# Hybrid attention block: block sums and feature squares move to PSUM and ScalarE, up operands are staged in PSUM, and the first chunk's weights get a buffer of their own

## The reference, cut to what matters

```python
u = rmsnorm(h, attn_norm_g[i])
proj = u @ w_in[i]
...                                   # oA: sliding-window attention, oB: differential attention
h = h + jnp.concatenate([oa, ob], axis=-1) @ w_out[i]
z = rmsnorm(h, mlp_norm_g[i]) @ w_up[i]
h = h + jnp.square(jax.nn.relu(z)) @ w_down[i]
gate = jax.nn.sigmoid(rmsnorm(h, ple_norm_g[i]) @ w_ple_gate[i])
h = h + gate * (p[i] @ w_ple_proj[i])
return rmsnorm(h, final_norm_g)
```

## Time and profile before

| what | value |
|---|---|
| median of 3 runs | 1267.04 us (1265.67 to 1267.32) |
| profiled execution, its own time | 1265.68 us |
| its span | 1263.9 us |
| mean granted PE clock | 0.988 |
| busy: PE, PE weight load, DVE, ACT, POOL | 96%, 76%, 62%, 38%, 48% of the span |
| one chunk, D3 to the next D3 | 81.26 us or 79.65 us |

### The profile page before, as it was taken

The page is one execution under the profiler, slowest core; times in us unless marked ns, Lnnn a source line. Parts: engine busy times, 40 slices in busy tenths (PEclk is TensorE's granted clock), DMA queues, the critical chain, the costliest instruction groups (busy, mean ns, idle before and its releaser), DMA issues.

```text
span 1263.9 us, 14541 instructions
## 1 busy us (share of the span) xinstructions
PE 1211.1 (96%) x5729; PEld 962.7 (76%) x5729; DVE 789.9 (62%) x958; ACT 481.5 (38%) x811; POOL 600.5 (48%) x269
## 2 busy tenths in 40 slices
PE   7999999999999997999999999999999999999997
PEld 5777777777677775778787787877878878888886
DVE  5254556556767597893947939579396693653223
ACT  7344435445555552222322223232232322342223
POOL 3220202222436575645666456654564656375641
PEclk8999999999999998999999999999999999999999
DMA  6811101112612324324234243252422514121203
GB/s 223 277 34 34 34 18 34 35 50 51 198 36 84 117 67 177 139 67 169 97 118 149 67 150 114 84 187 67 150 100 83 199 53 142 41 86 52 63 1 133
DMA packets 104121, 125.72 MB, mean 99 GB/s; under 512 B 21801, under 2 KB 87382, under 8 KB 98678
## 3 DMA queue, kind: packets, MB, share of 16 engines
q1 hardware_dynamic: 103814, 124.18, 30.1%
q10 hardware_dynamic: 240, 0.62, 0.1%
HBM read 111.14 MB, written 16.01 MB: 101 GB/s over the span
## 4 chain that ended last, share of the span: by engine, by line
PE 45%; DVE 10%; issue 5%; DMA 1%; POOL 0%; ACT 0%; SPq 0%; DVEq 0%; ACTq 0%
PE ps L1713 36%; PE ps L1374 8%; DVE block_raw L2337 4%; DVE h L2366 2%; DVE block_raw L2320 1%; DVE block_raw L2317 1%; PE ps L1398 1%; DVE w_raw L2262 1%; DMA raw_x<-in_w_up 1%; PE ps L1870 0%; PE ps L1412 0%; DVE diag L1957 0%; PE ps L1701 0%; POOL w_lo L832 0%; ACT w_hi L958 0%
## 5 line engine op out<-in xcount | busy, mean ns | idle before, releaser
L736 POOL TENSOR_TENSOR w_lo<-w_raw,w_hi 128x1024 fp32r<-128x1024 f32 x38 | 96.6, 2543 | 271.5 <-ACT w_hi L973 271.3
L832 POOL TENSOR_TENSOR w_lo<-w_raw,w_hi 128x1024 fp32r<-128x1024 f32 x57 | 142.7, 2504 | 163.5 <-ACT w_hi L958 159.7
L1713 PE MATMUL ps<-block_hi,w_hi 128*128 128x512 f32 x440 | 175.2, 398 | 20.9 <-DVE h L2366 14.0
L1713 PE MATMUL ps<-up_hi,w_hi 128*128 128x512 f32 x448 | 175.9, 393 | 9.4 <-DVE t_lo L2244 6.9
L1713 PE MATMUL ps<-block_lo,w_hi 128*128 128x512 f32 x472 | 183.7, 395 | 0.0
L1398 PE MATMUL ps<-u_hi,w_hi 128*128 128x512 f32 x416 | 177.1, 426 | 4.4 <-DVE o_bt L1982 1.7
L1713 PE MATMUL ps<-up_lo,w_hi 128*128 128x512 f32 x448 | 175.0, 391 | 0.0
L1713 PE MATMUL ps<-up_hi,w_lo 128*128 128x512 f32 x448 | 174.9, 390 | 0.0
L1713 PE MATMUL ps<-block_hi,w_lo 128*128 128x512 f32 x440 | 174.1, 396 | 0.0
L1398 PE MATMUL ps<-u_hi,w_lo 128*128 128x512 f32 x416 | 164.1, 394 | 0.0
L1398 PE MATMUL ps<-u_lo,w_hi 128*128 128x512 f32 x416 | 163.4, 393 | 0.0
(11 more groups left out here) (208 smaller groups left out, 2070.1 us busy)
## 6 DMA issues: line engine op xcount, KB each, us to landing
up_lo<-lo_save SPq DMA_DIRECT2D x36, 1024.0 KB, 5.8
w_raw<-in_w_in SPq DMA_DIRECT2D x48, 256.0 KB
w_raw<-in_w_down SPq DMA_DIRECT2D x18, 512.0 KB
raw_x<-in_w_up SPq DMA_DIRECT2D x16, 512.0 KB
w_raw<-in_w_up SPq DMA_DIRECT2D x16, 512.0 KB
raw_x<-in_w_down SPq DMA_DIRECT2D x14, 512.0 KB
x_raw<-in_x SPq DMA_DIRECT2D x8, 512.0 KB, 7.1
h_save<-x_t SPq DMA_DIRECT2D x1, 4096.0 KB, 12.7
```

The source lines that it names most:

```text
L736: nc.gpsimd.tensor_tensor(w_lo[:, s * D:(s + 1) * D], w_raw[:, s * D:(s + 1) * D], w_hi[:, s * D:(s + 1) * D].bitcast(F32), ALU.subtract). ...
L832: nc.gpsimd.tensor_tensor(w_lo[:, s * D:(s + 1) * D], raw, w_hi[:, s * D:(s + 1) * D].bitcast(F32), ALU.subtract).then_inc(lo_done, 1)
L1713: mm = nc.tensor.matmul(o, w, xx, start=(first and m == 0), stop=(last and m == 2), skip_group_check=onto)
```

## The change

- `hidden` is one DVE instruction now: relu(z)·rstd. The squaring is a new ACT instruction, `square_hidden`, from SBUF to SBUF, except that B12's square is written to the PSUM pair `d`. `rstd` for this is mean to the power -1/2, where it was -1 (POOL, one instruction as before).
- `block_sum`: T1 is made in place in pair `d`, T2 in pair `third`, both in PSUM; T3 and T4 go to SBUF tiles with one operand from PSUM. The order on DVE is T3, T1, T2, then B21's `hidden`, rests of T1 and T2, and T4 last. Rests of T1 and T2 read PSUM.
- PE's waits follow: D0's second half overwrites pair `d` and waits for T1's rest; D1 overwrites `third` and waits for T4.
- The up sums are written to PSUM banks 0, 1, 4, 5 (`T_BANK`), B12's gained half to banks 2, 3, 2, 5. T1 of a group is made one projection earlier than T2 to T4. ACT's roundings of T2 to T4 of a group stand behind the next weight rounding. U1 waits for 15 low parts instead of 16, U2 for all 16.
- `load_a12(0)` goes to a new tile `first_a12` and is issued before the last output weights, behind the last attention maximum. In chunk 0 ACT rounds U4's weights ahead of taking rstd.

```diff
@@ SP
             load_a22(0)
+            sp.wait_ge(a_m, N_SLOT)
+            load_a12(0)
...
+            sp.wait_ge(t_lo, 13)
+            save_lo(1, up_lo[:, 2 * T:4 * T])
             sp.wait_ge(t_lo, 16)
-            save_lo(1, up_lo[:, 2 * T:4 * T])
             save_lo(4, t4_lo[:, :])
-            sp.wait_ge(sq_ok, 2 * DT + 1)
-            load_a12(0)
@@ POOL
-                    nc.gpsimd.tensor_tensor(rs8[:, :], mean[:, :], mone[:, :], ALU.pow).then_inc(pow_ok, 1)
+                    nc.gpsimd.tensor_tensor(rs8[:, :], mean[:, :], mhalf[:, :], ALU.pow).then_inc(pow_ok, 1)
@@ ACT
+            def t_piece(i, n):
+                x = T_ORDER[n]
+                o = up_hi_at(x) + i * HALF
+                act.wait_ge(sums_raw, 4 * i + (n + 1 if x != T2 else 4))
+                nc.scalar.copy(up_hi[:, o:o + HALF], bank(T_BANK[x])).then_inc(sums_hi, 1)
...
+                if n % 2 == 0 and n:
+                    for m in range(1, 4):
+                        t_piece(n // 2 - 1, m)
...
+            def square_hidden(c, m, raw, to):
+                act.wait_ge(z_pos, 4 * c + m + 1)
+                nc.scalar.activation(to, raw[:, :], ACT.Square).then_inc(z_sq, 1)
@@ PE
                     if n < 2 and i in (0, 2):
-                        pe.wait_ge(z_sq, 4 * c + (1, 3, 2, 4)[2 * n + i // 2])
+                        if (n, i) == (0, 2):
+                            pe.wait_ge(op_lo, 7 * c + 2)
+                        elif (n, i) == (1, 0):
+                            pe.wait_ge(t_ok, 4 * c + 4)
+                        else:
+                            pe.wait_ge(z_pos, 4 * c + (1, 4)[n])
@@ DVE
                 nc.vector.scalar_tensor_tensor(out=to, in0=z, scalar=0.0, in1=r, op0=ALU.max,
                                                op1=ALU.mult).then_inc(z_pos, 1)
-                dve.wait_ge(z_pos, n + 1)
-                nc.vector.scalar_tensor_tensor(out=to, in0=z, scalar=0.0, in1=to, op0=ALU.max,
-                                               op1=ALU.mult).then_inc(z_sq, 1)
...
-                    block_sum(RAW[T1], B12_RAW, RAW[B11])
-                    dve.wait_ge(t_ok, 4 * c + 1)
-                    block_sum(RAW[T2], RAW[B22], RAW[T1])
+                d2, third2 = bank(2 * d, 2), bank(2 * third, 2)
+                block_sum(block_raw[RAW[T3]][:, :], r22[:, :], d2)
+                dve.wait_ge(t_ok, 4 * c + 1)
+                block_sum(d2, d2, r11[:, :])
+                dve.wait_ge(t_ok, 4 * c + 2)
+                block_sum(third2, r22[:, :], d2)
                 dve.wait_ge(blk_done, up_product(c, 6) + 1 - DONE0)
                 hidden(c, 3, b, 0, r21)
...
                 rest_of(c, 1)
-                block_sum(RAW[T4], RAW[B21], RAW[T2])
                 dve.wait_ge(t_ok, 4 * c + 3)
                 rest_of(c, 2)
+                dve.wait_ge(z_sq, 4 * c + 4)
+                block_sum(block_raw[RAW[T4]][:, :], r21[:, :], third2)
                 gather(c, 0)
```

More of the change, by code:

```diff
@@ L268, in bank, with b12_bank @@
             return ps[:, 512 * b:512 * (b + n)]
+        def b12_bank(i):
+            return bank((2, 3, 2, 5)[i])
         def y_banks(t):
@@ L475, in build @@
         B12_RAW, B11_LO = 1, 7
+        T_BANK = {T1: 0, T2: 1, T3: 4, T4: 5}
+        T_ORDER = (T1, T3, T2, T4)
+        r11, r12, r22, r21 = (block_raw[n] for n in (RAW[B11], B12_RAW, RAW[B22], RAW[B21]))
         LAST = 7 * (CHUNKS - 1)
@@ L1205, in _ @@
                 square_half(DT + n)
-                if n % 2:
-                    t_pieces(j - 4)
+                if n % 2 == 0:
+                    t_piece(j, 0)
+            for m in range(1, 4):
+                t_piece(3, m)
             def sum_hi(b, raw, ready, n):
@@ L1223, in round_down @@
                     act.wait_ge(blk_done, product(c, n - 3) + 1 - DONE0)
-                round_block(block_hi[n % 3], block_raw[RAW[(B11, T1, T2, B22, T3, T4, B21)[n]]], ready, count)
+                _, _, third, d = pairs_of(c)
+                if n in (1, 2):
+                    raw = bank(2 * (d if n == 1 else third), 2)
+                else:
+                    raw = block_raw[RAW[(B11, T1, T2, B22, T3, T4, B21)[n]]][:, :]
+                round_block(block_hi[n % 3], raw, ready, count)
             def copy_first(c):
@@ L1720, in lo_ready @@
                 x = UP[n]
+                if c == 0 and n == 0:
+                    pe.wait_ge(sums_raw, 10)
                 if x not in STREAMED:
@@ L1792, in _ @@
                     if (c, n) == (0, 2):
+                        pe.wait_ge(t_lo, 16)
                         sums(1, 5, acc_mlp)
@@ L2211, in gained_rest, with token_sum @@
                                                op0=ALU.mult, op1=ALU.subtract).then_inc(out_ok, 1)
-            def token_sums(i):
-                t1, t2, t3 = (raw[i][:, :] for raw in t_raw)
+            def token_sum(i, n):
+                x = T_ORDER[n]
+                out = bank(T_BANK[x])
                 g0, g4 = g_col[:, 8 + i:9 + i], g_col[:, 12 + i:13 + i]
@@ new lines, in token_sum, with sum_rest @@
+                nc.vector.scalar_tensor_tensor(out=out, in0=in0, scalar=g, in1=in1, op0=ALU.mult,
+                                               op1=op).then_inc(sums_raw, 1)
+            def sum_rest(i, n):
+                x = T_ORDER[n]
+                o = up_hi_at(x) + i * HALF
+                to = (up_lo_at(0, x) if x != T4 else 0) + i * HALF
+                dve.wait_ge(sums_raw, 4 * i + n + 1)
+                dve.wait_ge(sums_hi, 4 * i + n + 1)
+                nc.vector.tensor_tensor((t4_lo if x == T4 else up_lo)[:, to:to + HALF], bank(T_BANK[x]),
@@ L2366, in gather @@
                         nc.vector.tensor_tensor(hq, o, hq, ALU.add).then_inc(dn_free, 1)
-            r11, r12, r22, r21 = (block_raw[n] for n in (RAW[B11], B12_RAW, RAW[B22], RAW[B21]))
             for c in range(CHUNKS):
@@ L2388, in _ @@
                     dve.wait_ge(z_sq, 4 * c + 2)
-                    rest(LAST + 2, RAW[B22], RAW[B22], block_hi[1])
+                    rest(LAST + 2, RAW[B22], r22[:, :], block_hi[1])
                 dve.wait_ge(blk_done, up_product(c, 5) + 1 - DONE0)
```

148 lines of the change are left out of this document (71 added, 77 removed).

## The result

| | before | after |
|---|---|---|
| median, same chip | 1266.41 us (1265.67 to 1267.32) | 1231.38 us (1231.18 to 1232.18) |
| span of the profiled execution | 1263.9 us | 1230.4 us |
| mean granted PE clock | 0.988 | 0.995 |

The ratio is 0.9724, 95% interval 0.9707 to 0.9741. The change makes the kernel 35.0 us faster, where I forecast 33.

The account below looks back on a forecast made before the run. PE, busy 96% of the span, sets the time, so only its waits and slow stretches can shrink. 23 us in chunks, 9.6 ahead and 0.2 in the last chunk make 33 us: 1234 us, range 1228 to 1244.

Parts of the forecast that it names:

- 23 + 0.2: Chunks: seven full ones lose 7 instead of 30 us, gaining 23; the last gains 0.2 by ACT's square replacing a DVE instruction.
- The bound above (2.3): Chunks: each block sum with a PSUM operand takes 2.3 us instead of 1.23 if it waits for POOL after all.
- rival (d): Chunks: sums, rests and T4 slow down touching PSUM pairs while PE writes others; 1291 us, chance 0.03.
- The walk through the chunk: Chunk 3: D0's middle loses 0.6 us, D1 0.3, D3 does not wait; about 1.0 us lost per chunk instead of 3.4.
- rival (b): Before D3: POOL is next late in every chunk, about 1 us × 7; 1241 us, chance 0.2.
- Rival (a): Chunks: the clock still falls, two close waits counting like one; 1240 us for four chunks, 1245 for seven; chance 0.12.
- Ahead of chunk 0: Output projections to U4, and in chunk 0: 3.1 + 4.4 + 0.8 + 2.0 - 0.7 = 9.6 us gained, bounds 5 and 12.
- The gain of 3.1 us for POOL's waits: Last output projections: three waits for POOL go, as weight roundings now stand in front; 3.1 us with restarts.
- that of 2.0 us for U4: Chunk 0: U4's wait for POOL goes, since ACT no longer rounds its weights behind rstd; 2.0 us gained.
- a slow stretch of 1.6 us: Behind U1's wait: slow PE matmuls remain, costing 1.6 instead of 2.4 us, a gain of 0.8.
- 0.7 us lost to the norm's chain: Chunk 0: mean, power and diagonal share the port with B22's rests; 0.7 us lost.
- Rival (c): Ahead of chunk 0: the sums gain nothing because PE's output bank comes free late; 1243 us, chance 0.08.

Follow-up runs that it names:

- chunks_only: The kernel before with the change inside the chunks alone, everything ahead of chunk 0 as before: 1241.91 us.
- hold3: The changed kernel with three idle DVE reductions ahead of the gather of D1 in each of seven chunks, so D3 waits again: 1239.99 us.
- hold4: The changed kernel with four idle DVE reductions ahead of the gather of D1 in each of seven chunks: 1253.38 us.
- ahead_only: The kernel before with only the change ahead of chunk 0 and U3's own buffer; chunks as before: 1257.38 us.
- t1_third: The changed kernel with T1 summed first into PSUM pair `third` and T2 in an SBUF tile: 1225.06 us.
- squares_act_sums_sbuf: The changed kernel with squares still on ACT, but all block sums in SBUF with DVE's order and the waits of before: 1254.45 us.
- t1_third_ahead: `t1_third` with ACT's last-group roundings ahead of its gained copy and half square, and the mean ahead of B22's last rests: 1223.93 us.
- shared_a12: The changed kernel with U3's weights in chunk 0 back in the tile shared with the squares of h, behind the saves: 1231.59 us.
- squares_dve_sums_psum: The changed kernel with block sums still in PSUM, but the squares back on DVE as second instructions: 1239.61 us.

## Why the prediction was right

**What bounds the kernel.** The sum of PE's waits and slow stretches was the right account. From chunk 0's D0 to the eighth chunk's the traces differ by 24.3 us, where I had 23 + 0.2. (`chunks_only` measured 25.3; its trace has 24.3 too, and the kernel before beside it had a median 1.5 us above the execution that I read.)

**Sums and rests from PSUM at 1.23 us.** Right, 1.22 to 1.23, and this is where most of the gain comes from: 17.8 us alone, near half of it through the clock. The bound above (2.3) and with it rival (d) are out. The rule of 120 fixed cycles from PSUM instead of 58 (the Trainium skill, VectorE: DVE Perf Modes, section on the TRN2 errata) isn't borne out here: a rest of this shape takes 1.22 us from PSUM, and 1.22 or 1.23 from SBUF when POOL is idle.

**The square at 1.05 us.** 1.03 to PSUM, 1.06 to 1.07 within SBUF. DVE waits 1.10 us for it, as walked through.

**The walk through the chunk.** D0's middle I had at 0.6, it loses 0.48 + 0.10; D1 I had at 0.3, it loses 0.30 + 0.07. The period is 77.16 us, predicted 77.2. Before D3 POOL's low part ends at 761.39, and D3 starts at 761.98: the slack is 0.6 us, predicted 0.3, so rival (b) didn't come. One thing in between I had wrong: `sum_s3` takes 3.41 us beside POOL, not 1.2, but it runs beside `sum_s4` and not behind it, and ends when I said.

**The clock.** The two short waits of a chunk don't count like one long one; every window behind them is 1.00. Rival (a) is out, and `hold3` says by how much: a third wait of 1.05 us in the same chunk leaves the clock up as well. The Trainium skill, TensorE: Matmul & The Clock Gate, section on HAM oscillation, tells of a kernel that waits some 3 to 5 us for a DMA ahead of each tile and is throttled in every one; no wait of the chunks is that long here, and `hold4` with its 2.0 us lost the clock in three of seven.

**Ahead of chunk 0.** 9.6 predicted, 9.8 measured in `ahead_only`. That execution loses the clock at one D3 more than the one before; in the traces of the part itself, from one and the same matmul of the output projections (at 420.77 before, at 421.77 after) to chunk 0's D0, it is 101.68 us before and 91.39 after, 10.3 less. That this is near 9.6 is partly luck, for the terms moved inside it. The gain of 3.1 us for POOL's waits and that of 2.0 us for U4 came as said: these waits are gone. Two terms were mis-sized, in opposite directions:

- U1 waits 2.46 us (I said 2.6), but I let a slow stretch of 1.6 us remain out of 2.4, and there is none in the changed kernel's profile. The 2.4 stands in no row: before, the stretch cost 1.8 us (25 matmuls from 481.93). So the gain is 1.7 us, not 0.8. The same wait goes either way: in four profiled executions (the changed kernel, `t1_third`, `hold4`, `squares_act_sums_sbuf`) the clock stays up behind it, in five (`t1_third_ahead`, `shared_a12`, `hold3`, `ahead_only`, `squares_dve_sums_psum`) it falls. First the changed kernel, then `shared_a12`, in the 8 us behind U1's start:

```profile
475.00:483.00 8.00, 7.93 (x43) 6.87 (x44) 8.00 (x7) 3.00 (x4) 5.59 (x4) 1.00 0.33 136
```

```profile
475.00:483.00 8.00, 8.00 (x38) 6.65 (x36) 7.66 (x7) 1.53 (x3) 3.94 (x3) 0.79 0.68 246
```

- I had 0.7 us lost to the norm's chain, which would share the port with B22's rests. PE waits 1.60 us in all for the diagonal where it waited 0.28 before: 1.3 us lost. But the chain is no later: `diag` ends 17.1 us behind U1's start, and 17.5 before. It has both inputs in SBUF, begins 0.06 us behind POOL's `sum_s4` and takes 3.40 us, as it did before. What is new is that PE, with its clock up, gets there 1.7 us sooner behind U1's start. `diag` before and after, then POOL:

```profile
496.05 3.40 DVE L1957 TENSOR_TENSOR diag<-ident,rs 128x1024 f32<-128x1024 f32 x1 [3.83 <-POOL rs L890]
```

```profile
488.79 3.40 DVE L1991 TENSOR_TENSOR diag<-ident,rs 128x1024 f32<-128x1024 f32 x1 [1.76 <-POOL rs L895]
```

```profile
488.73 2.38 POOL L854 TENSOR_TENSOR s_sum<-first_a,w_raw 128x1024 f32<-128x1024 f32 x1
```

These two hide each other. In the executions in which the clock stays up behind U1, PE's wait for `diag` is 1.4 us; in those in which it falls, PE comes later and the wait is 0.2 us, or none where the mean is taken early. So the sum of the two hardly depends on the clock: the way from that matmul to chunk 0's D0 is 91.4 us in the four executions with the clock up and 91.8 or 91.9 in four of the five with it down (91.35 in `t1_third_ahead`).

**One step failed without a price.** I said that POOL's chain holds U1, 0.5 us behind DVE's. POOL's low part does end at 475.02, but DVE's last rest ends at 475.06 and releases PE. The two are as good as level, here and in `t1_third_ahead`, and DVE has no gap before its last rest, so its chain would hold U1 by itself.

**Another step failed, too.** I said that U3's weights, needed 8 us earlier, are brought by their own buffer. `shared_a12` shows that the shared tile would do: the last square of h and the saves are earlier as well, since the sums are. It cost nothing because I had put no term on it; had I worked out when the old transfer would be issued and land (475.6 and 480.4, against a need at 481.7), I would have seen that the edit isn't needed.

**Rival (c)** didn't come: PE has no wait for an output bank in the last projections.

## What to carry to other kernels

When a VectorE instruction beside GpSimd work takes twice its time or more, look whether both its inputs are in SBUF; one of them in a PSUM bank that happens to be free made it independent here. Alone, with the order that it allows, it was worth 17.8 us, against 2.9 for moving work to a less busy engine, while the two together gave 5 us more than their sum. When waits shrink, ask what the clock gives back as well: near a third of the 26.0 us here. Put the sum that is needed first into a bank whose content no later sum reads: this gave another 6.3 us. Before giving a transfer a buffer of its own, work out when it would be issued after the rest of the change.

## What the runs showed of the hardware

- PE's granted clock stayed at 1.00 behind recurring waits with steps 0.5, 1.05 and 1.89 us too long (seven of seven each), and fell to a mix of 0.79, seen over 8 us, behind 15 of 28 steps 2.2 us too long (2.0 us of idle PE) and behind five of nine of 2.46 us. A fall cost 1.6 us. I had not expected waits of the same length and place to part like this, in two kernels (`hold4`, `squares_act_sums_sbuf`) every second chunk. What decides it is open.
- DVE with one input in PSUM and POOL ran side by side with neither slowed (1.23 and 2.40 us), even where DVE's output and its other input are in SBUF (the rest at 748.50).
